# The decays' activation, running sums and rows of a two-block network issued as a lane of their own among the first head's products

## The chip, the cores and the metric

One core of one Trainium2 chip runs the whole program. The metric is the device time of that core in microseconds, from the start to the end of the program. TensorE (PE) multiplies matrices, VectorE (DVE) and ScalarE (ACT) do element work, GpSimd (POOL) a little of it, and SyncE (SP) issues the DMAs. Each engine works through its own list of instructions in order and waits on semaphores that the others raise.

## The reference

Input is one sequence of 512 tokens with 1024 features, in float32. The first block computes, with `h = rms_norm(x)`:

```python
(aq, ak, av, az, dq, dk, dv, db, da, dz, gate_att, gate_dn) = split_cols(h @ w_in)
o_att = gqa_attention(rope(norm(aq)), rope(norm(ak)), av)     # 8 heads, 2 key heads
y_att = (o_att * silu(az)) @ w_br_att
qkv   = silu(short_conv([dq, dk, dv], conv_w))                # 5 taps per channel
g     = -exp(a_log) * softplus(da + dt_bias)                  # 2 directions x 8 heads
beta  = sigmoid(db)
o_dn  = bidir_gated_deltanet(q, k, v, g, beta)                # uses cumsum(g) within a chunk
mix   = (sigmoid(gate_att) * y_att + sigmoid(gate_dn) * y_dn) @ w_out
```

A per-layer embedding gate follows, and then a second block of two layers (stick-breaking attention, differential attention, each with a gated feed-forward part). The change touches only how `g` and `beta` are computed and spread. Together they are 32 columns of `h @ w_in` and some arrays of 128 x 64 numbers.

## The kernel before, in words

All large products run as three fp32r passes per 128x128 block of weights (high x high, high x low, low x high), each over 512 tokens. The weights come as a stream of 1 MB pieces ("pairs" of 16 blocks); ACT makes the high half (`w_hi`) and DVE the low half (`w_lo`) of each.

A planner in Python, `Order`, writes down one global list of steps, and each engine's program is that list filtered for its part (`arrange`, from line 231; the engines' parts from `sync`, `tensor`, `vector`, `scalar` and `gpsimd`). The planner keeps an estimated clock for each engine. `o.main(...)` places a step at once, at the clock of PE. A lane is a generator that was handed to `o.spawn`. `o.step()` is called after the multiplications of a product; it goes through the lanes in the order of `PRIORITY` and advances one if the lane's own time is not after the clock of PE, and if the engines that its last `yield` named are at most 1.0 (`SLACK`) ahead of PE. `o.add` then places the lane's step at the lane's time and advances the clocks by the costs in `cost`. So the costs do not change what an instruction does; they decide where it stands in every engine's queue. A multiplication of a product has cost 0.228 (`MUL`), and it is placed in the same list.

The stage around the change comes after the first key products and the value product, at about 44 to 62 us of the trace:

- `gate_mm` (PE at line 1606, DVE at 2036): 24 multiplications with 32 columns of weights, a copy to SBUF by DVE (line 2038), four transposes to a second PSUM bank (line 1622).
- `gate_act` (ACT at 2536, DVE at 2039): exponential, sigmoid and softplus on 128x64 arrays. Its steps go back and forth between ACT and DVE and end with `gate_raw` (line 2056).
- `gate_cum` (PE at 1625, DVE at 2057, ACT at 2546): the sums within a chunk, as nine small float32 multiplications with a triangle or ones as weights (two records each in the trace). PE waits for `gate_raw` first. Then a copy (2060), two exponentials and a subtraction.
- `gate_t` (PE at 1633, DVE at 2065): four transposes, and the copy to `GS` (2067).
- `g_row` and two `g_ld` (SP at 1499 and 1503): the 16 rows go to DRAM, and a row for each direction comes back spread over 128 partitions.

Then the eight heads begin. For each, the main path has the products for k, q (attention), q (delta rule), the attention's gate, v and, from the second head on, more; lanes do rotation (`rope_lane`), attention, convolution, preparation (`prep_lane`), scan and gates. The readers of the decays are `pr_g` (line 2119, 2601) in `prep_lane`, `pr_kk`, and the scan. The stage uses one PSUM bank (`obank_att`) that attention's output takes later and one (`scan_bank`) that the scan takes later. A pair's `w_hi` steps are placed before blocks 3, 5, 7 and 9 of the pair before it, its `w_lo` steps before blocks 4, 6, 8 and 10.

Of the kernel before, what the change touches and what calls it, by code (L numbers as in the profile page):

```python
# [32 lines left out]
for _n, _w in (("norm_pre", 8), ("norm_post", 8), ("ple_norm", 8), ("attn0", 8), ("attn1", 8), ("ffn0", 8),  # L33
# [14 lines left out]
MARGIN = 0.0  # L48
SLACK = 1.0
MARGIN_1 = 0.0  # L50
PRIORITY = {"silu": -3, "egat": -3, "att": -2, "conv": -1, "con2": -1, "scan": 0, "out": 1, "prep": 2, "gate": 3, "load": 4, "halv": 4,
            "rope": 5}


# [66 lines left out]
class Order:  # L121
# [61 lines left out]
    def step(self, force=False):  # L183
        moved = False
        names = sorted(self.lanes, key=lambda n: PRIORITY.get(n[:4], 3))
        for name in names:
# [44 lines left out]
def arrange(o, n_pairs):  # L231
# [104 lines left out]
    def banked(kind, *key, cost, hold=False, bank=None):  # L336

        u = (bank or ring).take()
        st = o.add(kind, *key, cost=cost, u=u)
        if not hold:  # L340
            (bank or ring).give(u)
        return st
# [4 lines left out]
    u = ring.take()  # L347
# [52 lines left out]
    obank_att, scan_bank = Banks(o, [side[3]]), Banks(o, [side[4]])  # L400
    u, u2 = obank_att.take(), scan_bank.take()
# [1 line left out]
    st.u2 = u2  # L403
    obank_att.give(u)
    scan_bank.give(u2)
    o.step()
    o.main("gate_act", cost=[("AC", 3.0), ("DV", 2.0)])
    o.step()
    u = obank_att.take()
    o.main("gate_cum", cost=[("PE", 1.0), ("AC", 1.0), ("DV", 1.0)], u=u)  # L410
    obank_att.give(u)
    o.step()
    u = scan_bank.take()
    o.main("gate_t", cost=[("PE", 0.5), ("DV", 0.7)], u=u)
    scan_bank.give(u)
    o.add("g_row", cost=[("DMA", 2.0)])
    t_row = o.now
    for d in range(2):
        o.now = t_row
        o.add("g_ld", 0, d, cost=[("DMA", 3.0)])  # L420


    ua_slots, dz_slots = Slots(2), Slots(2)
# [4 lines left out]
    def att_lane(hd):  # L428
        while ("ar_out", f"q{hd}") not in o.at:
            yield  # L430
        o.behind(o.at["ar_out", f"q{hd}"])
        iq, uo = o.at["ar_out", f"q{hd}"].iq, None
        for qb in range(5):
            hint = "AC DV PE"
            yield hint
            while not ring.ready((qb > 0) + (qb < 4)):
                yield hint
            if qb > 1:
                while not uo and not obank_att.ready():
                    yield hint  # L440
                uo = uo or obank_att.take()
                o.behind(o.at["at_t", hd, qb - 2])
                o.add("at_o", hd, qb - 2, cost=[("PE", 0.9)], u=uo)
            t = max(o.now, o.at["at_n", hd, qb - 1].t) if qb else o.now
            if qb:
                banked("at_t", hd, qb - 1, cost=[("PE", 0.45), ("AC", AC_B)])
                o.now = t
            if qb < 4:
                banked("at_s", hd, qb, cost=[("PE", PE_B), ("DV", DV_B), ("AC", AC_B)]).iq = iq
                yield "DV"  # L450
                o.add("at_n", hd, qb, cost=[("DV", 0.15), ("DV", 0.5)])
        o.behind(o.at["at_t", hd, 3])
        yield "PE"
        o.add("at_o", hd, 3, cost=[("PE", 0.9)], u=uo)
        yield "DV"
        q_slots.give(iq, o.at["at_s", hd, 3])
        while ("az_out", hd) not in o.at:
            yield "DV"
        o.behind(o.at["az_out", hd])
        st = o.add("at_m", hd, cost=[("DV", DV_B)])  # L460
        st.u, st.i = uo, o.at["az_out", hd].i
        ua_outs[st.i] += 1
        st.out_n = ua_outs[st.i]
        obank_att.give(uo)
        ua_slots.give(st.i, st)
# [88 lines left out]
    def prep_lane(hd):  # L554

        while ("cv_n", 8 + hd) not in o.at or ("cv_n", hd) not in o.at:
            yield
        while not work.ready():
            yield
        _, w_old = work.take()  # L560
        ikeep, k_old = kept[hd]
        o.behind(w_old, o.at["cv_n", hd], o.at["cv_n", 8 + hd])

        def add(kind, *key, cost, ring_=True, hold=False):
            st = banked(kind, *key, cost=cost, hold=hold) if ring_ else o.add(kind, *key, cost=cost)
            st.hd, st.keep, st.k_old, st.w_old = hd, ikeep, k_old, w_old
            return st

        for d in range(2):
            o.behind(o.at["g_ld", hd, d])  # L570
            yield "DV"
            add("pr_g", hd, d, cost=[("AC", AC_B), ("DV", 4 * DV_S)], ring_=False)
            if hd < 7:
                t = o.now
                o.add("g_ld", hd + 1, d, cost=[("DMA", 4.0)])
                o.now = t
            yield
            add("pr_e", hd, d, cost=[("AC", AC_B), ("PO", PO_B), ("PO", PO_B)], ring_=False)
            yield "PE"
        while not ring.ready(2):  # L580
            yield "PE"
        st = add("pr_kk", hd, cost=[("PE", 1.7), ("DV", 2 * DV_B), ("DV", 8 * DV_S), ("AC", 1.2)], hold=True)
        st.u2 = ring.take()
        ring.give(st.u)
        ring.give(st.u2)
        yield
        add("lv_0", hd, cost=[("PO", 0.8), ("PO", 0.8), ("DV", 0.4), ("DV", 0.3)], ring_=False)
        for s in range(1, 5):
            yield "PE"
            while not ring.ready():  # L590
                yield "PE"
            add("lv_m", hd, s, cost=[("PE", 0.35), ("AC", 0.4)]).s = s
            yield "PE"
            while not ring.ready():
                yield "PE"
            add("lv_x", hd, s, cost=[("PE", 0.35), ("DV", 0.4), ("DV", 0.35)]).s = s
        add("lv_e", hd, cost=[("AC", 1.2), ("DV", 0.8)], ring_=False)
        yield "PE"
        while not ring.ready():
            yield "PE"  # L600
        add("lv_p1", hd, cost=[("PE", 0.25), ("AC", 0.3)])
        yield "PE"
        while not ring.ready(2):
            yield "PE"
        st = add("lv_p2", hd, cost=[("PE", 0.3), ("DV", 1.2)], hold=True)
        st.u2 = ring.take()
        ring.give(st.u)
        ring.give(st.u2)
        yield "PE"
        while not ring.ready():  # L610
            yield "PE"
        add("lv_q1", hd, cost=[("PE", 0.25), ("AC", 0.4)])
        yield "PE"
        while not ring.ready():
            yield "PE"
        st = add("lv_q2", hd, cost=[("PE", 0.25), ("DV", 0.5)])
        work.give(0, st)
# [76 lines left out]
    for hd in range(8):  # L694
        o.spawn("att", att_lane(hd))
        o.spawn("prep", prep_lane(hd))
        o.spawn("scan", scan_lane(hd))
        o.until(pads.ready)
        gemm(h, KT, conv_done(8 + hd))
        gemm(h, KT, a_rope(f"q{hd}"))  # L700
        o.until(pads.ready)
        gemm(h, KT, conv_done(hd))
        o.until(ua_slots.ready)
        gemm(h, KT, z_done("az", hd, ua_slots))
        o.until(pads.ready)
        gemm(h, KT, conv_done(16 + hd))
        if hd:
            o.until(lambda: not dz_slots.held[(hd - 1) % 2])
            gemm(h, KT, z_done("dz", hd - 1, dz_slots))
            if hd <= EARLY:  # L710
                gemm(h, KT, early_done(hd - 1))
        if hd == 7:
            o.until(lambda: not dz_slots.held[1])
            gemm(h, KT, z_done("dz", 7, dz_slots))
# [561 lines left out]
def build(nc, wstream, wba, consts, vecs, cossin, pos, xT, pT, outT):  # L1276
    n_pairs = wstream.shape[0]
    order = Order()
    arrange(order, n_pairs)
    steps, at = order.steps, order.at  # L1280

# [1766 lines left out]
```

## Time and profile before

| | us |
|---|---|
| three runs of the kernel before | 2298.47, 2302.9, 2304.11 (median 2302.9) |
| the profiled execution, its own time | 2299.77 |
| its span in the profile | 2298.0 |
| PE busy | 2200.8 (96%) |
| DVE busy | 1189.3 (52%) |
| ACT busy | 1011.5 (44%) |

The time of the profiled execution is 1.8 us more than its span, and 3.1 us less than the median of the three runs. PE is busy nearly all the time, so a microsecond counts where PE is idle or its clock is low.

### The profile page before, as it was taken

The page shows a single profiled execution, that of the slowest core. Times are in us where ns is not written, and L with a number is a line of the kernel's source. Part 1 is how long each engine was busy: PE and PEld are TensorE (multiplying, and loading weights), DVE is VectorE, ACT ScalarE, POOL GpSimd, SP SyncE. Part 2 cuts the span into 40 slices and gives each one's busy share as a digit, 9 for nine tenths or more (in the row PEclk, how much of TensorE's full clock was granted, in tenths as well). Part 3 has the DMA queues.
Part 4 walks back from the last instruction along what each step waited for, and adds up shares of the span by engine and source line. Part 5 has one row for each costly group of instructions (what it writes and reads, how often), then busy time and mean ns, then how long its engine had stood idle before and what let it go on. Part 6 is the DMA issues. An engine that isn't in the chain of part 4 may idle for free.

```text
span 2298.0 us, 35314 instructions
## 1 busy us (share of the span) xinstructions
PE 2200.8 (96%) x14886; PEld 1696.2 (74%) x14886; DVE 1189.3 (52%) x2101; ACT 1011.5 (44%) x1919; POOL 247.9 (11%) x273
## 2 busy tenths in 40 slices
PE   6999999999999999899999999999999989999999
PEld 4777776777777877686656888888876556888887
DVE  5566666666644446532335553444557665443442
ACT  4565656556554236534554331233445544331331
POOL 0022121221120011102221000001001001000000
PEclk9999999999999999999999999999999989999999
DMA  4221221221214332121111322232221112322232
GB/s 169 70 97 57 70 71 52 85 83 61 66 62 139 132 137 79 53 71 55 37 35 63 110 92 92 94 108 92 74 74 45 39 38 66 107 92 92 92 104 80
DMA packets 34766, 185.79 MB, mean 81 GB/s; under 512 B 4000, under 2 KB 4384, under 8 KB 15408
## 3 DMA queue, kind: packets, MB, share of 16 engines
q1 hardware_dynamic: 34608, 183.53, 23.6%
q8 instruction: 118, 1.93, 0.3%
q14 instruction: 40, 0.33, 0.0%
HBM read 172.99 MB, written 7.90 MB: 79 GB/s over the span
## 4 chain that ended last, share of the span: by engine, by line
PE 86%; DVE 7%; ACT 3%; issue 2%; DMA 1%; POOL 0%; SPq 0%; POOLq 0%; DVEq 0%; ACTq 0%
PE ps L1549 85%; PE ps L1552 1%; ACT arena L2439 1%; DVE spl L1989 1%; DMA on_t<-spill 0%; DMA arena<-arena 0%; DMA raw<-wstream 0%; DVE x L2316 0%; DVE arena L2139 0%; DVE x L2095 0%; ACT spl L2442 0%; ACT arena L2442 0%; ACT hh L2439 0%; DVE arena L2178 0%; DVE hl L2284 0%
## 5 line engine op out<-in xcount | busy, mean ns | idle before, releaser
L1549 PE MATMUL ps<-hh,spl 128*128 128x512 f32 x3232 | 1070.2, 405 | 28.4 <-DVE arena_r L2216 7.8
L1549 PEld LDWEIGHTS ps<-hh,spl 128*128 128x128 f32 x3232 | 606.2, 189 | 185.2 <-issue 41.5
L1549 PE MATMUL ps<-hl,spl 128*128 128x512 f32 x1552 | 629.4, 406 | 0.0
L1989 DVE TENSOR_TENSOR spl<-raw,spl 128x512 fp32r<-128x512 f32 x596 | 409.4, 713 | 171.8 <-ACT spl L2442 170.9
L1549 PE MATMUL ps<-arena_r,spl 128*128 128x512 f32 x1936 | 475.1, 401 | 9.7 <-DVE arena_r L2216 4.6
L1549 PEld LDWEIGHTS ps<-arena_r,spl 128*128 128x128 f32 x1936 | 366.3, 190 | 106.5 <-DVE arena_r L2220 6.5
L2442 ACT ACTIVATE spl<-raw 128x512 fp32r<-128x512 f32 x596 | 342.2, 618 | 142.1 <-PE ps L1549 140.9
L1549 PEld LDWEIGHTS ps<-hl,spl 128*128 128x128 f32 x1552 | 293.4, 189 | 73.9 <-issue 18.4
L1549 PE MATMUL ps<-arena 32*32 32x32 f32 (+7 forms) x5664 | 217.3, 224 | 18.7 <-DVE arena L2178 6.5
L2439 ACT ACTIVATE arena<-arena 128x512 f32<-128x512 f32 (+3 forms) x211 | 139.7, 663 | 190.7 <-DVE arena L2321 141.5
L1549 PEld LDWEIGHTS ps<-arena 32*32 32x32 f32 (+4 forms) x5664 | 126.2, 115 | 104.9 <-issue 76.6
L1549 PE MATMUL ps<-arena,cst 128*128 128x512 f32 (+3 forms) x308 | 111.4, 487 | 18.4 <-DVE arena L1996 13.9
L2442 ACT ACTIVATE arena_r<-arena 128x512 fp32r<-128x512 f32 x60 | 37.8, 631 | 201.7 <-DVE arena L2328 191.6
L2439 ACT ACTIVATE arena<-ps,small 128x512 f32<-128x512 f32 (+3 forms) x121 | 68.8, 571 | 126.6 <-PE ps L1549 71.5
L2439 ACT ACTIVATE arena<-ps 128x512 f32<-128x512 f32 (+3 forms) x92 | 60.9, 668 | 143.5 <-PE ps L1549 139.3
L2316 DVE TENSOR_TENSOR x<-x,ps 128x512 f32<-128x512 f32 x64 | 43.8, 684 | 146.8 <-PE ps L1549 146.8
L2864 POOL TENSOR_TENSOR arena<-arena 128x512 f32<-128x512 f32 x30 | 38.8, 1295 | 660.2 <-ACT arena L2439 660.2
L1549 PE MATMUL ps<-spl,hh 128*128 128x256 f32 x576 | 108.8, 290 | 0.0
L1549 PEld LDWEIGHTS ps<-spl,hh 128*128 128x128 f32 x576 | 89.9, 191 | 5.5 <-issue 4.9
L2325 DVE TENSOR_TENSOR arena<-ps,arena 128x512 f32<-128x512 f32 x44 | 30.4, 692 | 104.3 <-PE ps L1549 104.3
L1549 PEld LDWEIGHTS ps<-arena,cst 128*128 128x128 f32 x308 | 54.4, 197 | 40.6 <-issue 24.9
L1549 PE MATMUL ps<-spl,hl 128*128 128x256 f32 x288 | 81.4, 283 | 0.0
(216 smaller groups left out, 1904.6 us busy)
## 6 DMA issues: line engine op xcount, KB each, us to landing
raw<-wstream SPq DMA_DIRECT2D x149, 1024.0 KB, 5.0
GS<-g_rows SPq DMA_DIRECT2D x16, 256.0 KB, 3.3
spill<-x SPq DMA_DIRECT2D x14, 256.0 KB, 2.1
arena<-spill SPq DMA_DIRECT2D x12, 256.0 KB, 5.0
arena<-arena SPq DMA_DIRECT2D x20, 128.0 KB, 2.6
on_t<-spill SPq DMA_DIRECT2D x10, 256.0 KB, 2.9
x<-xT SPq DMA_DIRECT2D x4, 512.0 KB, 6.7
spill<-arena SPq DMA_DIRECT2D x8, 256.0 KB, 2.0
```

The costliest lines, as they stand in the source:

```text
L1549: return pe.matmul(out, lhsT, rhs, start=start, stop=stop, skip_group_check=True)
L1552: return pe.transpose(out, in_, C["ident"])
L1989: tt(spl[:, p % 2, 1, c], raw[:, p % 2, c], spl[:, p % 2, 0, c].bitcast(F32), ALU.subtract) \
L2316: tt(X[q.m], X[q.m], psum[q.u.b][:, :], ALU.add).then_inc(drained[q.u.b], 1)
L2325: tt(p, psum[q.u.b][:, :], SQ[q.g.name][2], ALU.mult).then_inc(drained[q.u.b], 1)
L2439: return act.activation(out, in_, func, **kw)
L2442: return act.activation(out, in_, ACT.Copy)
L2864: tt(acc, acc, tmp[q.i], ALU.add).then_inc(sem("sq_pool"), 1)
```

## The change

`gate_mm` stays where it is. What follows it is no longer placed by `o.main` ahead of the heads, but by a lane named "decay", with the highest priority (-4), which `o.step()` advances among the multiplications of the first head's products. Its costs are written anew. Two guards are added: attention's output bank is not taken before `gate_cum` is placed, and `prep_lane` doesn't ask for its decays before `g_ld` is placed. The instructions that the steps issue, and their waits, are the same ones.

```diff
-PRIORITY = {"silu": -3, "egat": -3, ...
+PRIORITY = {"deca": -4, "silu": -3, "egat": -3, ...
...
-    o.step()
-    o.main("gate_act", cost=[("AC", 3.0), ("DV", 2.0)])
-    o.step()
-    u = obank_att.take()
-    o.main("gate_cum", cost=[("PE", 1.0), ("AC", 1.0), ("DV", 1.0)], u=u)
-    obank_att.give(u)
-    o.step()
-    u = scan_bank.take()
-    o.main("gate_t", cost=[("PE", 0.5), ("DV", 0.7)], u=u)
-    scan_bank.give(u)
-    o.add("g_row", cost=[("DMA", 2.0)])
-    t_row = o.now
-    for d in range(2):
-        o.now = t_row
-        o.add("g_ld", 0, d, cost=[("DMA", 3.0)])
+    def decay_lane():
+        o.behind(o.at["gate_mm",])
+        yield "AC DV"
+        o.add("gate_act", cost=[("AC", 2.2), ("DV", 0.5)])
+        yield "PE"
+        u = obank_att.take()
+        o.add("gate_cum", cost=[("PE", 2.2), ("DV", 0.6), ("AC", 0.5)], u=u)
+        obank_att.give(u)
+        yield "PE"
+        u = scan_bank.take()
+        o.add("gate_t", cost=[("PE", 0.5), ("DV", 0.7)], u=u)
+        scan_bank.give(u)
+        o.add("g_row", cost=[("DMA", 2.0)])
+        t_row = o.now
+        for d in range(2):
+            o.now = t_row
+            o.add("g_ld", 0, d, cost=[("DMA", 3.0)])
+
+    o.spawn("decay", decay_lane())
...
-                while not uo and not obank_att.ready():
+                while not uo and (("gate_cum",) not in o.at or not obank_att.ready()):
...
         for d in range(2):
+            while ("g_ld", hd, d) not in o.at:
+                yield
             o.behind(o.at["g_ld", hd, d])
```

## Rows read from the trace of the kernel before

**Rows 1.** The page's totals, and the shares of the chain that ended last.

```profile
span 2298.0 us, 35314 instructions
...
PE 2200.8 (96%) x14886; PEld 1696.2 (74%) x14886; DVE 1189.3 (52%) x2101; ACT 1011.5 (44%) x1919; POOL 247.9 (11%) x273
...
PE 86%; DVE 7%; ACT 3%; issue 2%; DMA 1%; POOL 0%; SPq 0%; POOLq 0%; DVEq 0%; ACTq 0%
```

**Rows 2.** Waits of PE, 53 to 62 us: waited for, total, times, longest.

```profile
PE ps L1549 <- DVE small L2054: 3.0, 1, 3.0
PE ps L1622 <- DVE arena L2038: 0.8, 1, 0.8
PE ps L1552 <- DVE small L2060: 0.4, 1, 0.4
```

**Rows 3.** Timeline, 53 to 65 us: start, length, what, idle before.

```profile
53.49 0.43 PE L1622 MATMUL ps<-cst,arena 32*128 32x32 f32 x4 [0.77 <-DVE arena L2038]
...
56.42 0.43 DVE L2054 SCALAR_TENSOR_TENSOR small<-small 128x16 f32<-128x16 f32 x4
...
60.57 0.23 DVE L2060 COPY small<-ps 128x64 f32<-128x64 f32 x1 [3.72 <-PE ps L1549]
...
60.94 1.01 PE L1552 MATMUL ps<-cst,small 128*16 128x128 f32 x4 [0.41 <-DVE small L2060]
61.60 0.77 PE L1549 MATMUL ps<-hh,spl 128*128 128x512 f32 x1
...
64.77 0.39 PE L1549 MATMUL ps<-hh,spl 128*128 128x512 f32 x1
```

**Rows 4.** Stretches, 49 to 66 us: length, busy (count) by engine, granted clock, DMA.

```profile
49.00:51.00 2.00, 2.00 (x11) 0.91 (x9) 0.00 (x0) 0.00 (x0) 0.00 (x0) 1.00 0.00 0
53.00:56.90 3.90, 0.43 (x4) 0.32 (x4) 2.71 (x13) 1.10 (x5) 0.00 (x0) 1.00 0.00 0
56.90:57.50 0.60, 0.59 (x5) 0.60 (x6) 0.00 (x0) 0.00 (x0) 0.00 (x0) 0.96 0.00 0
57.50:60.90 3.40, 3.03 (x15) 2.84 (x14) 0.23 (x1) 0.07 (x1) 0.00 (x0) 0.50 0.00 0
61.60:64.00 2.40, 2.40 (x8) 1.91 (x7) 2.01 (x4) 1.63 (x4) 0.00 (x0) 0.50 0.09 21
64.30:66.00 1.70, 1.70 (x9) 1.38 (x8) 1.47 (x3) 0.00 (x0) 0.00 (x0) 1.00 0.15 59
```

**Rows 5.** Timeline of PE, 88 to 91 us: transposes and products at the full clock.

```profile
88.33 0.40 PE L1549 MATMUL ps<-hl,spl 128*128 128x512 f32 x1
88.58 0.63 PE L1552 MATMUL ps<-cst,arena 128*128 128x128 f32 x4
88.97 0.72 PE L1549 MATMUL ps<-hh,spl 128*128 128x512 f32 x2
```

**Rows 6.** Timeline of DVE and ACT: the last halves before, and the decays' first reader.

```profile
38.47 3.59 DVE L1989 TENSOR_TENSOR spl<-raw,spl 128x512 fp32r<-128x512 f32 x4
...
61.57 1.65 ACT L2442 ACTIVATE spl<-raw 128x512 fp32r<-128x512 f32 x3
...
117.59 0.87 DVE L2123 TENSOR_SCALAR arena<-GS,small 128x128 f32<-128x128 f32 x4
```

**Rows 7.** Waits of SP, 0 to 140 us, same columns as Rows 2.

```profile
SPq L1502 <- DVE GS L2067: 17.0, 1, 17.0
```

**Rows 8.** Stretches of the eight heads and of all behind them, columns as Rows 4.

```profile
61.60:700.00 638.40, 612.18 (x7702) 473.35 (x7701) 402.03 (x825) 376.95 (x758) 129.49 (x144) 1.00 0.21 71
700.00:2298.00 1598.00, 1550.02 (x6988) 1192.98 (x6987) 755.80 (x1212) 608.32 (x1114) 113.07 (x118) 0.98 0.24 82
```

**Rows 9.** Waits of PE, 61.6 to 700 us, same columns as Rows 2.

```profile
PE ps L1549 <- DVE arena L2178: 6.5, 7, 1.2
PE ps L1549 <- issue: 4.1, 8, 1.1
PE ps L1549 <- DVE arena L2035: 2.9, 1, 2.9
```

More of the change, by code:

```diff
@@ L50 @@
 MARGIN_1 = 0.0
-PRIORITY = {"silu": -3, "egat": -3, "att": -2, "conv": -1, "con2": -1, "scan": 0, "out": 1, "prep": 2, "gate": 3, "load": 4, "halv": 4,
+PRIORITY = {"deca": -4, "silu": -3, "egat": -3, "att": -2, "conv": -1, "con2": -1, "scan": 0, "out": 1, "prep": 2, "gate": 3, "load": 4, "halv": 4,
             "rope": 5}
```

## Prediction

> **What bounds the kernel now.** I read the page's totals first. PE is busy for 2200.8 of 2298.0 us and makes up 86% of the chain that ends last [rows 1]. So only three kinds of time can change: PE's idle time, PE's work at its lower clock, and the work itself. Next I asked who PE waits for around the edited stage. There it sits idle three times: 0.8 us before the four small transposes, 3.0 us before the sums, 0.4 us before the last transposes [rows 2]. The timeline shows what lies in the longest of these: the transposes of `gate_mm` end at 53.92 (53.49 + 0.43), and the last of the small ACT and DVE steps that work on their result ends at 56.85 (56.42 + 0.43) [rows 3]. No large product is placed ahead of the sums, so PE has nothing else to do. The first product of the first head starts at 61.60 [rows 3].
>
> The third view is the granted clock. The sums start at the full clock, and from 57.5 us on PE has half of it (0.50, that is 1.2 of 2.4 GHz), through the rest of the sums, the transposes and the first products until about 64; from 64.3 it has 1.00 again [rows 4]. What PE did before the fall is the 2.99 us of idleness and a stretch of tiny multiplications. So the stage costs twice: by waits and by slow work behind them.
>
> Last I looked at what comes after. In the eight heads PE is idle for 638.40 - 612.18 = 26.2 us, in the rest for 1598.00 - 1550.02 = 48.0 us [rows 8]. What the lanes of the heads cost is that 26.2 us, in single waits of 0.5 to 2.9 us [rows 9].
>
> **The change part by part.** It issues the same instructions, in another place. I compare the time from 53.92 us, when the transposes of `gate_mm` end, to 64.77 us, when the ninth multiplication of the first head starts [rows 3]: 10.85 us. In it lie eight multiplications, the eighteen records of the sums, and four transposes. With the clock full and no wait the same work would take:
>
> - the sums: 5 records in 0.60 us just before the clock falls [rows 4], so 0.12 us each, and 18 x 0.12 = 2.16 us. From below, the nine products could not be cheaper than that row; from above, it is what they took at the half clock, 15 records in 3.40 us or 0.23 each, 4.1 us [rows 4]. I take 2.16, since the row of the full clock is the one that fits if PE isn't idle.
> - the transposes: four took 0.39 us between products (88.58 to 88.97) [rows 5]. I take that; from below I know nothing cheaper, and from above stands the 0.66 us that they took here (60.94 to 61.60) [rows 3].
> - eight products: 9 records in 1.70 us, less the parts cut by the window, agree with 0.23 each [rows 4]; 88.33 to 88.58 shows 0.25 with a change of kind behind it [rows 5]. 8 x 0.23 = 1.84 us.
> - four changes between products and small work: 0.02 us each by that row, so 0.1 in all; bounds 0 and 1.0, as if the whole 0.25 were a change.
>
> The sum is 2.16 + 0.39 + 1.84 + 0.1 = 4.5, and 10.85 - 4.5 = 6.4 us (rounded) are gained. Of these 3.3 are idleness (3.0 + 0.4, less 0.1 for the changes) [rows 2], and 3.1 come from the clock.
>
> Does the stall go, or only move? The lane puts `gate_act` first in the queues of ACT and DVE, after some two products, and `gate_cum` once the plan's PE is past its end. By the plan's costs that is 2.2 + 0.5 and two hops of 0.08, 2.86, and 2.86 / 0.228 gives the thirteenth multiplication. In the trace thirteen take 13 x 0.23 = 2.99 us and PE is at the sums at about 56.95, while their data are ready at 56.85 [rows 3]. So the margin is only 0.1 us. What is late next is PE itself, if nothing cuts in on ACT or DVE. The next thing placed there is the high half of the next pair, of about 0.55 us (three in 1.65) [rows 6]. It is placed before block 3, behind `gate_act` in ACT's queue; if it were in front, PE would wait up to 0.5 us. Behind PE's wait would then stand the products, so it would count in full. For `gate_t` the plan waits six multiplications, 1.4 us, for a copy that took 0.23 us (60.57 to 60.80) [rows 3]; no wait is left there (0.4 before). I count 0 and keep 0.5 as the bound.
>
> Weights: the products now start at 53.9 instead of 61.6. The halves that they need were done at 42.06 (38.47 + 3.59) [rows 6]. The next pair's halves were made from 61.57 on only because ACT stood behind the decays' last exponential; they are needed 48 multiplications after the start, 11 us and the lane's own 2.6, so at about 67.5. ACT and DVE are nearly empty until then. Cost 0, and a bound of 1 us if the last of the four halves, placed behind the first evacuation, comes late.
>
> The moved DMAs: one `g_row` and two `g_ld`, issued by SP. SP waited 17.0 us for the row [rows 7]. It has nothing else to issue then, and the next load of weights is placed far behind. The row's copy will come at about 60 us against 62, and the first reader of `GS` starts at 117.59 [rows 6], so more than 50 us cover it. The rotation of the first query goes behind these DMAs on SP as before. The two guards cost nothing: attention and `prep_lane` begin after the lane has ended. Cost 0; without the cover it would be whatever the row is late, and it is early.
>
> Behind the clock's term stands this: PE has the full clock in the 32-column products, through their 0.8 us of idleness and through the 3.0 us, and falls 0.6 us behind those [rows 2, 4]. The Trainium skill has a rule that speaks against my reading: "TensorE: Matmul & The Clock Gate", part 4 on the transpose, says that transposes don't count as PE activity in the way matmuls do. By it the two sets of four transposes, so close to the tiny multiplications, could pull the clock down in spite of the products between them; the sum would be 3.3 us by it and 6.4 without it. In the trace the transposes between products at 88 us run at the full clock's pace [rows 5], but they are few among many products.
>
> The sum is made for the profiled execution: 2299.77 - 6.4 = 2293.4 us. That execution is 3.1 us under the median of the runs, so for the median I forecast 2302.9 - 6.4 = 2296.5 us.
>
> **The rivals.**
>
> *The clock falls anyway.* Then only the idleness goes, 3.3 us, and the time is 2299.6 us. For it speaks that the sums are 2 to 4 us of multiplications with 8 columns. Against it, the fall came after the idleness, not with the 32-column work. One in ten.
>
> *It is given back.* The first head's lanes start from other plan clocks, so from here to the end of the heads the steps of ACT, DVE and POOL are placed a little differently, and PE's 26.2 us of waits are drawn anew. If they grow by the 3 to 9 us of one to three waits like the 2.9 us behind L2035 [rows 9], the result lies within 3 us of the old time, about 2302. For it: that wait belongs to a rotation whose DMA and DVE steps stand in a full queue. Against it: most waits are below 1.2 us each. Fifteen in a hundred.
>
> *Slower.* One mechanism: the output of the rotation (L2035), which attention's first scores and with them all of PE's queue wait for, is placed behind more convolution and halving steps on DVE in most heads, not in one. It costs 2.9 us each time [rows 9]. From three such waits on it exceeds the gain; with six more it is 17.4 - 6.4 = 11 us slower, 2314 us. For it: nothing in the plan knows of real lateness. Against it: one head of eight has it now. Twelve in a hundred.
>
> *More than the stage.* The new placement closes waits in the heads as well. If a third of the 26.2 us goes, 9 us more, the time is 2288 us. Thirteen in a hundred.
>
> *The change does nothing*, because the lane is placed so late that its order equals the old one: excluded by the priority, as the lane comes first at each step and attention waits for it.
>
> **How the numbers follow.** The forecast, with 3 to 10 us gained, has one in two; the clock's rival 0.10, given back 0.15, slower 0.12, more 0.13. About 0.3%, or 6.9 us, is what a measurement of this kernel tells from no change. The gain of 6.4 lies just inside this. Of the forecast's 0.50 I put 0.28 above 6.9, with the 0.13 that makes 0.41 for faster. Slower by over 6.9 us needs 13 us of new waits: 0.09 of the 0.12. The rest, 0.50, is no change. The range goes from 2287 (a third of the waits gone, and a bit more) to 2305 (the gain and 2 us more given back), which leaves about 2 in 10 outside.
>
> **What would show it.** In the changed kernel's timeline products follow the transposes of `gate_mm` at once; PE's waits for L2054 and L2060 are gone or below 0.5 us; the sums' 18 records take about 2.2 us; the granted clock is 1.00 from 54 to 66 us; and the four halves of the next pair are made between 56 and 65. PE's idle time in the heads stays at 26 us, give or take 5. I am wrong if the clock is 0.50 among the first products, if PE waits at the sums for more than 1 us, or if the idle time of the heads moves by more than the 6.4 us.

## The result, and the profile after

| kernel | median of runs, us | ratio to before, 95% interval |
|---|---|---|
| before | 2303.35 (6 runs) | |
| changed | 2293.22 (6 runs, 2290.51 to 2295.10) | 0.9958 [0.9946, 0.9970] |

The change makes the kernel faster by 10.1 us by the medians, 0.42% by the ratio. The forecast was 2296.5 us and a range of 2287 to 2305. I had given "no change" 0.50 and "faster" 0.41, with 6.9 us as the line between them; the measured gain lies beyond that line, and the lower end of its interval (0.9970, 6.9 us) lies on it. The profiled execution of the changed kernel has a span of 2292.6 us against 2298.0, which is 5.4 us less. Single executions of one kernel differ by some us (2298.47 to 2305.66 for the kernel before), so I read what a stage does from the traces and the total from the medians.

PE in the changed kernel, 53 to 62 us: start, length, what, idle before. It answers to [rows 3].

```profile
53.86 0.43 PE L1630 MATMUL ps<-cst,arena 32*128 32x32 f32 x4 [0.77 <-DVE arena L2046]
54.22 0.50 PE L1557 MATMUL ps<-hh,spl 128*128 128x512 f32 x1
...
56.85 0.61 PE L1557 MATMUL ps<-hh,spl 128*128 128x512 f32 x2
57.30 2.21 PE L1557 MATMUL ps<-small,cst 128*128 128x8 f32 x18
59.32 0.48 PE L1557 MATMUL ps<-hl,spl 128*128 128x512 f32 x1
...
60.80 0.60 PE L1560 MATMUL ps<-cst,small 128*16 128x128 f32 x4
61.15 0.48 PE L1557 MATMUL ps<-hl,spl 128*128 128x512 f32 x1
```

The first head's products start right behind the transposes of `gate_mm`. Between 54.22 and the sums stand thirteen of them, then six, then the last transposes. No bracket stands behind the sums or the last transposes: those two waits are gone. The eighteen records of the sums take 2.21 us. This execution ran 0.37 us late before the stage (53.86 against 53.49). The last decay step of DVE in the same trace shows the margin at the sums:

```profile
56.80 0.43 DVE L2062 SCALAR_TENSOR_TENSOR small<-small 128x16 f32<-128x16 f32 x4
```

It ends at 57.23, and PE comes at 57.30. The granted clock is the value ahead of the DMA share (columns as [rows 4]); it stays at 1.00 through the whole stage, where it had been 0.50 from 57.5 us on:

```profile
53.00:66.00 13.00, 12.23 (x67) 10.14 (x67) 8.74 (x25) 4.99 (x13) 0.00 (x0) 1.00 0.04 14
57.30:59.40 2.10, 2.10 (x20) 2.10 (x20) 1.82 (x3) 0.00 (x0) 0.00 (x0) 1.00 0.00 0
61.20:66.00 4.80, 4.80 (x23) 3.97 (x22) 3.34 (x6) 2.33 (x4) 0.00 (x0) 1.00 0.10 33
```

The PE waits of the changed kernel from 60 to 700 us answer to [rows 9]. The wait of 2.9 us for the rotation's output is not among them; the waits for DVE's low halves have grown to 3.6 us from 1.3, and those for one more line of DVE (L2092, L2084 in before) to 3.4 from 1.0.

```profile
PE ps L1557 <- DVE arena L2186: 5.8, 8, 1.2
PE ps L1557 <- issue: 4.5, 7, 1.6
PE ps L1557 <- DVE spl L1997: 3.6, 3, 1.8
PE ps L1557 <- DVE arena L2092: 3.4, 2, 2.6
```

### The profile page after: what moved, and what is told of

It is laid out like the page before. It is cut to its first block, busy times and chain, and to the rows that moved or that the text cites. A ratio compares the mean times of both kernels' runs of the same rounds, so it can differ in the third digit from the quotient of the medians.

```text
span 2292.6 us, 35315 instructions
## 1 busy us (share of the span) xinstructions
PE 2198.6 (96%) x14886; PEld 1693.3 (74%) x14886; DVE 1194.4 (52%) x2101; ACT 1009.2 (44%) x1919; POOL 249.4 (11%) x273
## 4 chain that ended last, share of the span: by engine, by line
PE 86%; DVE 7%; ACT 3%; issue 2%; DMA 1%; POOL 0%; SPq 0%; POOLq 0%; DVEq 0%; ACTq 0%
PE ps L1557 84%; PE ps L1560 1%; ACT arena L2447 1%; DVE spl L1997 1%; DVE arena L2147 0%; DMA raw<-wstream 0%; ACT spl L2450 0%; DVE x L2324 0%; ACT arena L2450 0%; DVE hl L2292 0%; ACT hh L2447 0%; DMA on_t<-spill 0%; DVE arena L2141 0%; DVE arena L2186 0%; DVE x L2288 0%
```

## The experiments

To measure what the heads add, I use one landmark behind them, the issue of the DMA that loads the input `pT`. It stands behind all of the heads' lanes and in every trace once. The two times near the end of each line are those of the first and the last issue. These are before, changed, e1 and e5:

```profile
L1533 SPq DMA_DIRECT2D arena<-pT x1: 327/327/327, 769.9 to 769.9; - x1
```

```profile
L1541 SPq DMA_DIRECT2D arena<-pT x1: 328/328/328, 762.9 to 762.9; - x1
```

```profile
L1550 SPq DMA_DIRECT2D arena<-pT x1: 328/328/328, 763.8 to 763.8; - x1
```

```profile
L1541 SPq DMA_DIRECT2D arena<-pT x1: 327/327/327, 775.2 to 775.2; - x1
```

The landmark has a spread of its own. In three traces of the changed kernel it stands at 762.9, 761.5 (e4) and 762.2 (e12).

### The stage alone, and the order alone

e1 and e2 form a square with the two kernels. A small function after the planner takes the decay steps out of its finished list and puts them back behind a given number of multiplications. In e1 it works on the list of before, in e2 on the list of the changed kernel. It also puts one step of k's rotation (`ar_rot`) directly behind `gate_mm`; the list of before has it there already, that of the changed kernel one multiplication later.

```diff
-    steps, at = order.steps, order.at
+    steps, at = moved(order.steps, (2, 13, 19)), order.at   # e1, in before
...
+    steps, at = moved(order.steps, (0, 0, 0)), order.at     # e2, in the changed kernel
```

> The planner's list of before, with only the decay steps moved: gate_act behind 2, gate_cum behind 13, gate_t with its row and loads behind 19 multiplications of the first head. Every other step stands as in before. Theory A (the gain is the stage alone, 6.4 to 6.5 us, and the new order of the rest is worth nothing): 6 to 7 us faster than before, ratio 0.9972, and no different from the changed kernel by more than 2 us beyond noise. Theory B (part of the measured 10 us comes from the new order of the lanes in the eight heads): 6 to 7 us faster than before as well, but 3 to 4 us slower than the changed kernel. Theory C (the old order fits the earlier start badly): under 5 us faster.

> The changed kernel's list, with the decay steps moved back directly behind gate_mm; the order of all the rest is the changed one. Theory A: 6 to 7 us slower than the changed kernel, so equal to before within 2 us. Theory B: as much slower than the changed kernel, but 3 to 4 us faster than before, ratio 0.9985. In both, the trace shows PE's 3.0 and 0.4 us of waits again and the half clock from about 57 to 64 us.

> The changed kernel once more, beside the others. Both theories: within its interval, 6.9 to 12.4 us faster than before. If the true gain is the 5.4 us that the two profiles differ by, it comes nearer to 0.997; if it is the median's 10 us, 0.9957.

| | decay steps behind `gate_mm` | decay steps among the products |
|---|---|---|
| order of before | before: 1 | e1: 0.9969 [0.9957, 0.9981], 2294.37 us |
| order of the changed kernel | e2: 0.9993 [0.9984, 1.0001], 2300.73 us | e4: 0.9962 [0.9950, 0.9975], 2293.41 us |

The median of before beside them was 2301.35 us. Theory A fits best: e1 is 1.0 us from the changed kernel and e2 0.6 us from before, where theory B wanted 3 to 4 us, and theory C wanted less than 5 us of gain in e1. e2's trace has the waits of 3.0 and 0.4 us again and the half clock from 57.3 to 64.1 us. Moving the steps is worth 7.0 us in one order (2301.35 - 2294.37) and 7.3 us in the other (2300.73 - 2293.41). The new order of everything else is worth 0.6 us without the move and 1.0 us with it, and neither is clear of the measurement. At the landmark e2 stands 2.7 us ahead of before and e4 2.3 us ahead of e1, but the changed kernel's own traces spread over 1.4 us there, and e3 below, with the order of before, stands 3.0 us behind before. So the stage is shown as the cause of the bulk, and the order as worth nothing that can be told from the spread. The second and third measurements of the changed kernel (0.9962, and 0.9960 in e12) say that the gain is some 9 us by the ratios.

### What pulls the clock down

> The kernel before, with 13 extra multiplications (128x128 weights, 512 columns, fp32r, from the normed input into a PSUM bank nobody uses yet) on PE in its wait for the sums' data. They add nothing to the result; they only take away PE's idleness of 3.0 us. My theory (3.1 of the 6.4 us are the clock, which falls because of the idleness): the granted clock stays 1.00 from 54 to 66 us, the 18 records of the sums take 2.2 us instead of 3.6, and the kernel is 3.0 us faster than before (0.9987) though PE waits as long as ever for useful work. Rival (the clock falls because of the tiny multiplications or the transposes): the clock falls as before, no gain, or 0.1 us slower.

```diff
                 elif kind == "gate_cum":
+                    for j in range(13):
+                        mm(psum[7][:, :], hh[:, j % 8, 0:128], hh[:, (j + 1) % 8, :], True, True)
                     w.wait_ge(sem("gate_raw"), 1)
```

e3 took 2302.7 us, a ratio of 1.0002 [0.9993, 1.0011]: no gain, and my expectation of 3.0 us missed. The sums did run at the full clock, but the clock fell behind them:

```profile
54.67 3.24 PE L1549 MATMUL ps<-hh 128*128 128x512 f32 x13
57.75 2.20 PE L1549 MATMUL ps<-small,cst 128*128 128x8 f32 x18
60.36 0.99 PE L1552 MATMUL ps<-cst,small 128*16 128x128 f32 x4 [0.41 <-DVE small L2062]
61.01 0.78 PE L1549 MATMUL ps<-hh,spl 128*128 128x512 f32 x1
```

```profile
57.50:60.40 2.90, 2.49 (x21) 2.15 (x20) 0.40 (x4) 0.15 (x1) 0.00 (x0) 1.00 0.00 0
60.40:63.80 3.40, 3.40 (x11) 2.61 (x12) 2.73 (x6) 1.89 (x5) 0.00 (x0) 0.50 0.06 14
```

The 18 records take 2.20 us instead of 3.63, a gain of 1.4 us; the transposes and the products behind them still have the durations of the half clock (0.99 us for the four, [rows 3] had 1.01). The half clock lasts 3.4 us, where before had it for 6.8 (57.5 to 64.3). So the result lies between the two theories. What was gained here was lost later in the heads, whose order is that of before: the landmark stands at 772.9, 3.0 us later. Part of that is 3.4 us more at the lower clock (371.0 to 374.4 in e3, where before has 1.00); the rest is spread that no run explains. So the 3.0 us of idleness are not needed for the fall; 0.4 us of it were still there. e6 and e7 ask what else there is.

> As e1 (the order of before, decay steps moved), but the last transposes directly behind the sums, with no multiplications of a product between them. e3 showed the clock falling 3.4 us later than in before, behind the same sums and a wait of 0.4 us, although PE had been kept busy ahead of them. Theory D (the tiny multiplications, the wait and the transposes together pull the clock down, and the products of e1 between them prevent it): 0.4 us of wait, a half clock for 3.4 us from about 60 us on, so some 2 us slower than e1. Theory E (the clock falls only behind idleness of some us; e3's dummies merely delayed that): full clock, 0.4 us slower than e1.

> As e1, but the sums behind 8 instead of 13 multiplications and the transposes behind 14. The prediction put the margin at the sums at 0.1 us. By it PE arrives 5 x 0.23 = 1.1 us sooner and waits 1.0 to 1.1 us for the last decay step of DVE; the kernel is about 1.1 us slower than e1, if the clock holds. If a wait of 1.1 us is hidden elsewhere: equal to e1.

```diff
-    steps, at = moved(order.steps, (2, 13, 19)), order.at
+    steps, at = moved(order.steps, (2, 13, 13)), order.at   # e6
...
+    steps, at = moved(order.steps, (2, 8, 14)), order.at    # e7
```

e6 took 2296.09 us (0.9965 [0.9953, 0.9978]), 1.7 us more than e1's 2294.37 by the medians, in another set of runs. Its five executions lie between 2291.26 and 2299.35, e1's six between 2293.70 and 2295.96, so the times alone do not show e6 to be slower. In its trace PE sits idle for 0.4 us between the sums and the transposes, and the clock falls at about 60.6 us:

```profile
59.52 0.60 PE L1569 MATMUL ps<-cst,small 128*16 128x128 f32 x4 [0.41 <-DVE small L2077]
```

```profile
57.00:60.50 3.50, 3.09 (x26) 2.83 (x26) 1.36 (x5) 0.73 (x3) 0.00 (x0) 1.00 0.00 0
60.50:64.00 3.50, 3.50 (x10) 2.75 (x9) 2.89 (x5) 0.79 (x2) 0.00 (x0) 0.52 0.12 29
```

```profile
60.68 0.63 PE L1566 MATMUL ps<-hl,spl 128*128 128x512 f32 x1
...
64.30 0.39 PE L1566 MATMUL ps<-hl,spl 128*128 128x512 f32 x1
```

e7 took 2296.80 us (0.9973 [0.9963, 0.9984]), 2.4 us more than e1. PE waits 0.9 us for the last decay step, where the prediction's margin gives 1.0 to 1.1, and here too the clock falls, from 58.7 to 62, so the expected 1.1 us with a clock that holds was too little:

```profile
PE ps L1566 <- DVE small L2071: 0.9, 1, 0.9
```

```profile
58.70:62.00 3.30, 3.30 (x11) 2.29 (x11) 1.24 (x4) 2.04 (x5) 0.00 (x0) 0.50 0.02 5
```

Theory E has fallen: the clock falls with a wait of 0.4 or 0.9 us beside the tiny multiplications. All 14 traces sort the same way: the five with such a wait (before, e2, e3, e6, e7) have the half clock behind it, the other nine keep 1.00 through the stage. Of theory D the last transposes are not needed: in before the clock falls at 57.5 and in e7 at 58.7 us, and these transposes come only at 60.94 and 61.37. The clock's price in e6 can be read as well: nine multiplications start from 60.68 up to 64.30, in 3.62 us, where 0.23 each would be 2.07. That is 1.6 us, and with the wait 2.0 us, as theory D had it.

Two rows limit what may be made of this. In before PE is idle for 2.9 us at 131 us, between large products, and the clock does not fall:

```profile
131.00:138.00 7.00, 4.10 (x26) 3.20 (x24) 4.91 (x10) 5.24 (x11) 1.63 (x1) 1.00 0.61 187
```

And the same wait of 2.29 us, at the same place of the changed kernel, ends at the full clock in one execution and at half of it in another (the first trace, where it ends at 206.07, and e4, where it ends at 204.76):

```profile
204.60:212.00 7.40, 4.87 (x143) 3.79 (x144) 5.74 (x12) 5.54 (x11) 2.18 (x3) 1.00 0.01 2
```

```profile
204.60:211.40 6.80, 6.63 (x140) 5.16 (x141) 3.95 (x10) 4.24 (x9) 2.32 (x2) 0.50 0.01 2
```

So something that these rows do not show has a part in such a fall, and e6 and e7 have one trace each. That the wait matters rests on all 14 traces together.

### How much the order of the heads can cost

> The changed kernel, but its lane has the costs of the kernel before (3.0 and 2.0, then 1.0, 1.0, 1.0). The planner then places the sums behind 23 multiplications instead of 13, and the steps of the heads in yet another order. If the stage is all that counts and the exact place does not: PE waits nowhere at the sums or the transposes, no half clock before 200 us, and 6.5 to 7.5 us faster than before (0.997), as e1 and e4. If the order of the heads' lanes is worth several us, this third order comes out 3 us or more away from the changed kernel, to either side.

> e5 with the decay steps moved to where the changed kernel has them (behind 2, 13 and 19 multiplications); every other step keeps e5's order. e5 was about 10 us slower than e1, with a wait of 5.1 us for an evacuation by ACT into the convolution's pad and 5.9 us for DVE's low halves. Theory F (e5's loss is the order of the heads' lanes that the costs made): as slow as e5, 2302 to 2306 us, with the same waits. Theory G (it is the later place of the sums and transposes itself): as e1, 2294 to 2295 us.

```diff
-        o.add("gate_act", cost=[("AC", 2.2), ("DV", 0.5)])
+        o.add("gate_act", cost=[("AC", 3.0), ("DV", 2.0)])
...
-        o.add("gate_cum", cost=[("PE", 2.2), ("DV", 0.6), ("AC", 0.5)], u=u)
+        o.add("gate_cum", cost=[("PE", 1.0), ("AC", 1.0), ("DV", 1.0)], u=u)
```

The expectation named a distance of 3 us or more as one outcome, but the size is one that I did not foresee. With the same lane and only other numbers in `cost`, the kernel is slower than before: 2304.73 us, 1.0014 [1.0005, 1.0024]. e9, which has e5's order and the changed kernel's places for the decay steps, took 2304.48 us, 1.0015 [1.0006, 1.0024]. Its waits in the heads have e5's totals (6.0, 5.9 and 5.9 us for the first three). So theory F holds, and the place of the sums is not the reason. PE has no wait at the sums in e5; its waits in the heads are these (66 to 700 us):

```profile
PE ps L1557 <- ACT pad L2450: 6.0, 3, 5.1
PE ps L1557 <- DVE spl L1997: 5.9, 4, 2.9
PE ps L1557 <- DVE arena L2186: 5.9, 8, 1.2
PE ps L1557 <- issue: 4.5, 4, 2.3
```

The longest, 5.05 us, ends at 212.52, and ACT's timeline shows why:

```profile
209.63 1.69 ACT L2450 ACTIVATE arena<-arena 32x256 f32<-32x256 f32 x4 [3.80 <-DVE arena L2147]
211.35 0.63 ACT L2450 ACTIVATE spl<-raw 128x512 fp32r<-128x512 f32 x1
211.88 0.58 ACT L2450 ACTIVATE pad<-ps 128x512 f32<-128x512 f32 x1
212.36 0.62 ACT L2447 ACTIVATE x<-arena 128x512 f32<-128x512 f32 x1
```

```profile
212.52 0.80 PE L1557 MATMUL ps<-hh,spl 128*128 128x512 f32 x1 [5.05 <-ACT pad L2450]
```

The evacuation of a product's bank (`pad<-ps`) stands in ACT's queue behind four copies of the preparation. These wait 3.80 us for DVE, so PE's next product has no bank. In the changed kernel the copies wait even longer, and PE still loses only 2.3 us:

```profile
201.63 1.69 ACT L2450 ACTIVATE arena<-arena 32x256 f32<-32x256 f32 x4 [4.25 <-DVE arena L2147]
```

```profile
203.39 0.39 PE L1557 MATMUL ps<-hh,spl 128*128 128x512 f32 x1
206.07 0.50 PE L1557 MATMUL ps<-hh,spl 128*128 128x512 f32 x1 [2.29 <-ACT pad L2450]
```

What differs is where PE stands. There it runs out of products at 203.78, 2.1 us behind the start of the copies; in e5 it does so at 207.47, 2.2 us ahead of it.

The waits are not all of the loss. These are the stretches from 66 us to the landmark in e5 and in e1, with the same instructions of PE but for two records:

```profile
66.00:775.20 709.20, 675.23 (x7934) 518.62 (x7933) 432.97 (x871) 401.34 (x804) 130.19 (x144) 0.98 0.24 80
```

```profile
66.00:763.80 697.80, 668.47 (x7932) 516.86 (x7931) 428.15 (x868) 402.58 (x804) 129.59 (x144) 0.99 0.24 81
```

e5 takes 11.4 us more. PE is idle for 34.0 instead of 29.3 us, which is 4.6 of it, and busy for 6.8 us more. It is at the lower clock for 27.2 us (from 212.1, at the end of the wait of 5.05 us, to 215.5, and in five stretches more), e1 for 13.6. In e9's trace, with e5's order, PE is idle for 35.6 us and busy for 1.2 us more than in e1: the longer waits are there again, the longer time at the lower clock is not. The times of e9 and e12, from one set of runs, show how far apart two orders are: 2304.48 - 2291.29 = 13.2 us.

### One wait more

> The changed kernel, with the four transposes of gate_mm as a step of the lane too, among the first products, so that PE need not wait 0.77 us for DVE's copy. If that wait is worth itself: no wait between the 32-column products and the first head, 0.7 us faster than the changed kernel, which is at the edge of what five rounds can tell; the sums come 0.9 us later in the lane. If the new order of the heads costs or gives more than 2 us, the time shows that instead.

> The order of before as in e1, with the four transposes of gate_mm moved among the first products too (behind 4 multiplications; gate_act behind 5, sums behind 17, last transposes behind 23). e8 did the same in the changed kernel and came out 3 us better than e4, though only 0.8 us of wait goes. If the wait is all: 0.7 us faster than e1, 2293.7 us. If there is more to it (the clock, as PE is never idle there): 2 to 3 us faster than e1.

> e8 again, on one chip with the changed kernel. If its advantage is the wait of 0.77 us alone: 0.7 us under e12. If the 3 us that it stood apart from e4 are real: 2 to 3 us under e12.

> The changed kernel again, as the partner of e11 and e9 on the same chip: 8 to 10 us faster than before, as in its first two measurements (10.1 us by medians, then 7.9).

```diff
                     i.then_inc(filled[q.u.b], 1)
+                elif kind == "gate_tr":
+                    q = at["gate_mm",]
                     w.wait_ge(drained[q.u.b], q.u.n)
...
         o.behind(o.at["gate_mm",])
+        yield "PE"
+        o.add("gate_tr", cost=[("PE", 0.5)])
         yield "AC DV"
```

`gate_mm`'s cost loses its 0.4 for the transposes and has 0.8 for DVE in place of 1.2. In e8 the transposes stand behind four multiplications, without a wait:

```profile
52.99 0.39 PE L1559 MATMUL ps<-hh,spl 128*128 128x512 f32 x1
...
53.99 0.43 PE L1634 MATMUL ps<-cst,arena 32*128 32x32 f32 x4
54.35 0.50 PE L1559 MATMUL ps<-hl,spl 128*128 128x512 f32 x1
```

| | us | ratio to before |
|---|---|---|
| e8 | 2290.48 | 0.9944 [0.9931, 0.9958] |
| e11, the same kernel | 2290.80 | 0.9958 [0.9944, 0.9971] |
| e12, the changed kernel beside e11 | 2291.29 | 0.9960 [0.9947, 0.9972] |
| e10, split in the order of before | 2292.88 | 0.9965 [0.9953, 0.9978] |

Side by side, e11 is 0.5 us under e12, as a wait of 0.77 us would have it; the intervals overlap, so it is not shown to be faster. e8's 3 us came from another set of runs than its partner and weren't found again. e12 is 10.1 us under the 2301.42 us of before beside it, at the upper end of what was expected. e10 is 8.5 us under it, e1 was 7.0 us under its own partner; the 1.5 us between them, from two sets, settle nothing. The version with the split has the lowest medians of all, and its trace has no PE wait at the stage.

## Why the prediction was right, and where it was not

**What bounds the kernel.** Right: PE's idleness and its clock were the two costs, and e1 shows that the stage's place alone brings 7.0 us (4.4 to 9.9 by its interval).

**The sum.** The stage was put at 6.4 us. From the start of the four transposes of `gate_mm` to the twentieth multiplication of the first head, the changed kernel takes 61.15 - 53.86 = 7.3 us. In before the same work ends eleven multiplications behind 64.77, at 67.3, and takes 67.3 - 53.49 = 13.8 us. The difference is 6.5 us. Of the single terms, the sums were put at 2.16 us (2.21 measured), the four last transposes at 0.39 (60.80 to 61.15 is 0.35), the place at thirteen and six multiplications (so it is), PE's arrival 0.1 us behind its data (0.07). One reading was right by luck: the 3.40 us of the half clock hold 0.37 us of idleness, and two of the 15 records are also among the five before; 13 records in 3.03 us give the same 0.23. The total went further than the sum. I forecast 6.4 us and 10.1 were measured, and 6.4 lies just outside the interval of 6.9 to 12.4; the profiled execution, at 2294.88, came out 1.5 us above the 2293.4 that I had for it.

**The clock.** The size was right, the reason half wrong. I had the half clock follow from 3.0 us of idleness and gave the rival that it falls anyway one in ten. e3, e6 and e7 show that it falls without those 3.0 us, if the tiny multiplications have a wait of 0.4 or 0.9 us beside them. The rival's condition was nearer than I thought, and the placement by the costs 2.2, 0.6 and 0.5 avoids it by little. The rule of the Trainium skill that I weighed ("TensorE: Matmul & The Clock Gate", part 4, on the transpose) did not bring the clock down in the changed kernel: two sets of four transposes start there at 53.86 and 60.80 us, and the granted clock is 1.00 from 53 to 66. Nor does the fall need the last transposes, which come behind it in before and in e7. No run here takes the transposes away by themselves, so their share in e6's fall, and that of `gate_mm`'s four, is open.

**The moved DMAs and guards.** Counted at 0. No wait for `GS` appears among PE's in the changed kernel, and e1, with the same three DMAs moved, has its gain in full. The row's copy to `GS` came at 61.80 us, not at about 60 as I had it (61.99 in before); the first reader starts at 114.6, so the error costs nothing.

**The rest of the heads.** I took their 26.2 us of waits to stay, give or take 5. In the changed kernel they are 645.80 - 621.10 = 24.7 us:

```profile
54.20:700.00 645.80, 621.10 (x7752) 479.65 (x7751) 410.81 (x844) 377.91 (x768) 130.91 (x144) 0.99 0.21 70
```

The landmark stands 7.0, 8.4 and 7.7 us ahead of before's (762.9, 761.5, 762.2), against a stage of 6.5 us. Behind the landmark the profiled execution of the changed kernel takes 1.6 us more than that of before, which leaves the 5.4 us between their spans. The same three traces show how much of this is spread: from 66 us to the landmark PE is idle for 29.2, 25.4 and 26.6 us and at the lower clock for 10.2, 20.4 and 13.6 us, with the same instructions in the same order (before: 30.5 idle, 10.2 at the lower clock). So the change may have closed some waits of the heads, by 1 to 5 us, with part of it taken back by the clock. What put the result on the other side of my line can't be told: e1's 7.0 us lie beyond it without any new order, but with an interval of 4.4 to 9.9, and the rest up to 10.1 us is within the intervals. The weight of 0.50 on "no change" came from a forecast 0.5 us short of the line, not from doubt in the mechanism.

**The slower rival.** Its size was fair and its place wrong. I had it in repeated waits for the rotation's output, 2.9 us each. In e5 the loss against e1, 2304.73 - 2294.37 = 10.4 us by medians of two sets of runs, has other causes: one wait of 5.05 us behind ACT's blocked copies and 5.9 us for low halves (1.3 in before), in place of smaller waits, so that 4.6 us of idleness are added in all; and, in e5's trace, PE is busy for 6.8 us more, with 13.6 us more at the lower clock. I had priced the rival by waits alone. The gain of this change was thus not safe with the lane alone; its costs had to place the rest well too.

## What to carry to other kernels

A chain that goes back and forth between engines on tiny data cost PE twice here: its own latency, and slow work behind it. Put it among large products with a few of them between its PE parts, and look for the clock in the trace even where only 0.4 us of idleness is left. Where a planner writes the order, move the steps in its finished list once, with all else in place: it separates what a change does from what its new order does. Here the move brings 7 us, and an unlucky order (e5, e9) takes more than that.

## What the runs showed of the hardware that was not expected

With PE busy through the 3 us wait (e3), the granted clock still fell, at 60.4 us instead of 57.5. With 13 products ahead of the sums and 0.4 us of idleness behind them (e6) it fell at 60.6; with none (the changed kernel, e1, e5, e8) it did not fall before 200 us. Idleness alone did not do it: 2.9 us of it between large products (before, at 131 us) left the clock at 1.00. Executions of one kernel differ in where it falls and for how long: at the end of the same wait of 2.29 us it is 1.00 in one trace and 0.50 in another, and between 66 us and the landmark the three traces of the changed kernel are at the lower clock for 10.2, 20.4 and 13.6 us. The sums, nine float32 products of which eight have 8 columns and one 64, take 0.12 us per record at the full clock (18 in 2.2 us) and 0.23 at half of it (13 in 3.03 us, [rows 4]).
